# The MLP's down product as seven half-size block products

## The reference, cut to what matters

```python
h2 = rms_norm(x, norm_mlp[layer])
x = x + jnp.square(jax.nn.relu(h2 @ w_ff1[layer])) @ w_ff2[layer]
return rms_norm(x, norm_final)
```

## Time and profile before

| What | us |
|---|---|
| median of 3 runs | 1758.12 (1756.83 to 1758.76) |
| the profiled execution | 1756.69 |
| its span, first to last instruction | 1755.1 |
| TensorE matmul busy | 1740.4 (99%) |
| VectorE busy | 801.2 (46%) |
| ScalarE busy | 589.3 (34%) |
| GpSimd busy | 80.7 (5%) |

### The profile page before, as it was taken

One profiled execution on the slowest core, in us unless ns is written; L12 is line 12 of the kernel. 1 busy time (PEld: TensorE's weight loads), 2 busy tenths in 40 slices (PEclk: granted clock), 3 DMA queues, 4 the chain that ended last, 5 costly groups with the idle time before them and its releaser, 6 DMA issues.

```text
span 1755.1 us, 21871 instructions
## 1 busy us (share of the span) xinstructions
PE 1740.4 (99%) x8476; PEld 1275.0 (73%) x8476; DVE 801.2 (46%) x1160; ACT 589.3 (34%) x754; POOL 80.7 (5%) x148
## 2 busy tenths in 40 slices
PE   9999999999999999999999999999999999999998
PEld 7888888874444444444788877788888888888886
DVE  6323338453342424243672455566675544324423
ACT  5334433331212111122454534354532253113313
POOL 3000000000000000000020022200000000000000
PEclk9999999999999999999999999999999999999999
DMA  6222222858999999999314221222242222232232
GB/s 209 94 96 93 72 72 97 341 229 346 423 422 421 422 422 422 422 422 401 107 49 131 92 94 52 80 86 97 95 174 98 100 96 96 96 96 96 96 97 83
DMA packets 91169, 326.34 MB, mean 186 GB/s; under 512 B 8720, under 2 KB 9248, under 8 KB 66528
## 3 DMA queue, kind: packets, MB, share of 16 engines
q1 hardware_dynamic: 89328, 320.18, 48.1%
q0 software_dynamic: 1776, 5.26, 0.9%
HBM read 319.13 MB, written 6.29 MB: 185 GB/s over the span
## 4 chain that ended last, share of the span: by engine, by line
PE 97%; DVE 1%; ACT 1%; DMA 0%; issue 0%; SPq 0%; DVEq 0%; ACTq 0%
PE bank L2309 61%; PE bank L2640 13%; PE bank L2653 6%; PE bank L2548 3%; PE bank L2595 3%; PE bank L2334 3%; PE bank L2882 2%; PE bank L2820 1%; PE bank L2764 1%; PE bank L2841 1%; PE bank L2913 0%; PE bank L2511 0%; DMA w_stage<-in_w_in 0%; PE bank L2522 0%; PE bank L2919 0%
## 5 line engine op out<-in xcount | busy, mean ns | idle before, releaser
L2309 PE MATMUL bank<-act_hi,w_hi 128*128 128x512 f32 x992 | 389.7, 393 | 0.0
L2309 PE MATMUL bank<-act_hi,w_lo 128*128 128x512 f32 x992 | 386.3, 389 | 0.0
L2309 PE MATMUL bank<-act_lo,w_hi 128*128 128x512 f32 x992 | 386.2, 389 | 0.0
L1457 DVE TENSOR_TENSOR w_lo<-w_stage,w_hi 128x2048 fp32r<-128x2048 f32 x98 | 224.4, 2289 | 349.4 <-ACT w_hi L859 349.4
L859 ACT ACTIVATE w_hi<-w_stage 128x2048 fp32r<-128x2048 f32 x98 | 187.8, 1916 | 383.3 <-PE bank L2309 377.8
L2640 PE MATMUL bank<-ring,xgT 128*64 128x512 f32 x992 | 215.7, 592 | 0.2 <-ACT xgT L1078 0.2
L2309 PEld LDWEIGHTS bank<-act_hi,w_hi 128*128 128x128 f32 x992 | 186.3, 188 | 40.0 <-issue 2.5
L2309 PEld LDWEIGHTS bank<-act_hi,w_lo 128*128 128x128 f32 x992 | 186.2, 188 | 39.2
L2309 PEld LDWEIGHTS bank<-act_lo,w_hi 128*128 128x128 f32 x992 | 186.4, 188 | 37.6
L2640 PEld LDWEIGHTS bank<-ring,xgT 128*64 128x64 f32 x992 | 70.7, 137 | 141.5 <-issue 141.0
L2653 PE MATMUL bank<-ring,gatedT 128*64 128x512 f32 x512 | 113.4, 595 | 0.0
(11 more groups left out here) (430 smaller groups left out, 2035.7 us busy)
## 6 DMA issues: line engine op xcount, KB each, us to landing
ring<-in_w SPq DMA_DIRECT2D x188, 1024.0 KB, 12.0
w_stage<-in_w_in SPq DMA_DIRECT2D x45, 1024.0 KB, 5.0
w_stage<-in_w_ff SPq DMA_DIRECT2D x32, 1024.0 KB, 5.2
w_stage<-in_w_out SPq DMA_DIRECT2D x8, 1024.0 KB, 5.1
extra<-in_w SPq DMA_DIRECT2D x4, 1024.0 KB, 8.4
branch_gates<-gate_out POOLq DMA_DIRECT2D x16, 256.0 KB, 2.5
w_stage<-in_w_proj_gla SPq DMA_DIRECT2D x4, 1024.0 KB, 9.8
w_stage<-in_w_pg SPq DMA_DIRECT2D x3, 1024.0 KB, 5.1
```

The lines of the kernel that those rows point to most:

```text
L1457: dve.tensor_tensor(w_lo[s][:, 0:ktiles, :], w_stage[s][:, 0:ktiles, :], w_hi[s][:, 0:ktiles, :].bitcast(F32), ALU.subtract).then_inc(w_lo ...
L2309: ins = pe.matmul(gb[j][:, :], left, right, start=(kc == 0 and k == 0 and n_pass == 0), stop=(kc == g.chunks - 1 and k == g.ktiles - 1 and ...
```

## The change

The down product of each half is the product of A (512 tokens x 2048) and B (2048 x 1024). It's now cut in quarters: A into a11, a12 (tokens 0 to 255, hidden 0 to 1023 and 1024 to 2047) and a21, a22 (tokens 256 to 511), B likewise into b11, b12 (the first 1024 rows, columns 0 to 511 and 512 to 1023) and b21, b22. In place of eight products of quarters there are seven, in this order (PARTS = 7):

| part | left operand | right operand | bank pair, added into |
|---|---|---|---|
| 0 | a11 | b11 | gb[0:2], rows 0-255, first columns |
| 1 | a12 | b21 | mb[0:2], the same quarter |
| 2 | S2 = a21 + a22 - a11 | T2 = b22 - b12 + b11 | on top of part 0; rows 0-255, second columns |
| 3 | S1 = S2 + a11 | T1 = b12 - b11 | gb[2:4]; rows 256-511, second columns |
| 4 | S3 = a11 - a21 | T3 = b22 - b12 | on top of 2; rows 256-511, second columns |
| 5 | S4 = a12 - S2 | b22 | on top of 3; rows 0-255, second columns |
| 6 | a22 | T4 = b21 - T2 | on top of 4; rows 256-511, first columns |

Each part is two steps of one 1 MB weight block each (step v = 2 x part + kc, 14 steps a half), each step two tiles of 12 matmuls: 7 x 2 x 2 x 12 = 336 matmuls a half. After each part DVE adds its two banks into `x` (`add_part`), 14 additions a half.

- `hidden` now holds the squares in float32, written by DVE alone; ACT's squares are gone. Each part's left operand, 128 x 8 x 256, is split when it's needed (`part_split_hi` on ACT, `part_split_lo` on DVE) into a double buffer.
- The sums S1 to S4 are four DVE instructions of 128x2048 a half (`sum_three` in the up phase, the others in the down phase).
- The sums T1 to T4 are made of 1 MB blocks on GpSimd, ten instructions of 128x2048 a half (`summed_block`): sums 1 to 4 (for T2) in the up phase, 5 and 6 (T1), 7 and 8 (T3), 9 and 10 (T4) while the down product runs. The blocks that they need are loaded again, so a half loads 18 blocks for the down product where it loaded 8.
- Semaphores `lb_diff` and `gl_edge` are given up; their waits go by `const_dve` and `gl_dist`.
- At the end the halves of the final norm follow the order in which quarters are ready, and the last part holds only the first columns of row tiles 2 and 3.

```diff
+        part_bank = [(gb[0:2], mb[0:2], gb[0:2], gb[2:4], gb[0:2], gb[2:4], gb[0:2])[n] for n in range(PARTS)]
+        step_stage = (w_stage[0], w_stage[1], w_stage[0], b_one[1], b_sum[0], b_sum[1], w_stage[0], w_stage[1],
+                      b_one[1], b_one[0], b_one[1], b_one[0], b_sum[0], b_sum[1])
...
+                sp.wait_ge(w_lo_done, step(h, 1))
+                sp.dma_start(w_stage[1][:, :, :], weight_block(h, 1, 1, 1)).then_inc(w_loaded[1], 16)
+                sp.wait_ge(w_lo_done, step(h, 2))
+                sp.dma_start(w_stage[0][:, :, :], weight_block(h, 1, 1, 0)).then_inc(w_loaded[0], 16)
+                sp.wait_ge(w_lo_done, step(h, 3))
+                sp.dma_start(b_one[1][:, :, :], weight_block(h, 0, 0, 0)).then_inc(b_one_in[1], 16)
+                sp.wait_ge(part_low, PARTS * h + 3)
+                sp.wait_ge(hid_summed, 4 * h + S4)
+                sp.dma_start(b_one[0][:, :, :], weight_block(h, 0, 0, 1)).then_inc(b_one_in[0], 16)
...
+            def summed_block(out, left, right, op):
+
+                pool.tensor_tensor(out[:, :, :], left[:, :, :], right[:, :, :], op).then_inc(b_summed, 1)
...
+                for kc in (1, 0):
+                    pool.wait_ge(w_loaded[kc], stage0[kc] + (48, 32)[kc])
+                    summed_block(w_stage[kc], w_stage[kc], b_sum[kc], ALU.subtract)
+                for kc in range(2):
+                    pool.wait_ge(b_one_in[1 - kc], 16 * ((4, 5)[1 - kc] * h + (5, 4)[kc]))
+                    summed_block(b_one[1 - kc], b_sum[kc], b_one[1 - kc], ALU.subtract)
+                for kc in range(2):
+                    pool.wait_ge(w_loaded[kc], stage0[kc] + (64, 48)[kc])
+                    pool.wait_ge(w_lo_done, step(h, 4 + kc))
+                    summed_block(b_sum[kc], w_stage[kc], b_sum[kc], ALU.subtract)
...
+                act.wait_ge(pe_tiles, (down.chunk0 + v - 1) * 4)
+                act.activation(w_hi[v % 2][:, :, :], step_stage[v][:, :, :], ACT.Copy).then_inc(w_hi_done, 1)
...
+                step_split_lo(h, 1)
+                part_split_lo(h, 1)
+                step_split_lo(h, 2)
+                sum_two(h)
...
+                for n in range(PARTS - 2):
+                    step_split_lo(h, 2 * n + 3)
+                    part_split_lo(h, n + 2)
+                    add_part(h, n, 0)
+                    step_split_lo(h, 2 * n + 4)
+                    add_part(h, n, 1)
+                    if n == 0:
+                        sum_one(h)
+                    elif n == 1:
+                        sum_four(h)
...
+                for k in range(4):
+                    ka = 4 * kc + k
+                    for n_pass, (left, right) in enumerate(((a_hi, hi), (a_hi, lo), (a_lo, hi))):
+                        ins = pe.matmul(part_bank[n][j][:, :], left[:, ka, cols], right[:, k, :],
+                                        start=(part_first[n] and kc == 0 and k == 0 and n_pass == 0),
+                                        stop=(kc == 1 and k == 3 and n_pass == 2), skip_group_check=True)
+                ins.then_inc(pe_tiles, 2)
```

More of the change, by code:

```diff
@@ L35, with __init__ @@
 class Gemm:
-    def __init__(self, after, units, chunks, taker, ktiles=4):
+    def __init__(self, after, units, chunks, taker, ktiles=4, tiles=4):
         self.taker, self.after = taker, after
@@ L48, in __init__ @@
         self.chunk1 = self.chunk0 + units * chunks
-        self.tile1 = self.out[taker] = self.tile0 + 4 * units
+        self.tile1 = self.out[taker] = self.tile0 + tiles * units
 class Chain:
@@ L126, in two_blocks @@
         up = Gemm(last, FH // 512, 2, "act")
-        last = Gemm(up, 2, FH // 512, "dve")
+        last = Gemm(up, 2, PARTS, "dve", tiles=PARTS)
         g_ff.append((up, last))
@@ L689, in _ @@
             for t in range(NT):
-                for half, done, count in ((slice(512, D), n_xn, rows_count(6, t)), (slice(0, 512), last_left, NT + t + 1)):
+                for half, done, count in ((late(t), n_xn, rows_count(6, t)), (early(t), last_left, NT + t + 1)):
                     sp.wait_ge(done, count)
@@ L1387, in mlp_squares, with relu_unit @@
                                        accum_out=ssq[:, t:t + 1]))
-            def relu_unit(h, u, chunk):
+            def relu_unit(h, u):
+                up = g_ff[h][0]
                 for j in range(4):
[L1392 to L1402, removed]
+                    act.wait_ge(pe_tiles, (up.chunk0 + 2 * u + 1) * 4 + j + 1)
+                    if hid_count(h, u) + j >= 2:
+                        act.wait_ge(hid_sq, hid_count(h, u) + j - 1)
+                    act.activation(relu_t[j % 2][:, :], gb[j][:, :], ACT.Relu).then_inc(out_act, 1)
@@ L2233, in hidden_unit, with part_split_lo @@
                         .then_inc(hid_sq, 1)
[L2234 to L2239, removed]
+            def part_split_lo(h, n):
+                dve.wait_ge(part_high, PARTS * h + n + 1)
+                rest(part_lo[n % 2][:, :, :], part_operand[n], part_hi[n % 2][:, :, :]).then_inc(part_low, 1)
@@ L2241, in _, with sum_one, sum_four @@
+            def sum_one(h):
+                dve.wait_ge(hid_summed, 4 * h + S2)
+                dve.tensor_tensor(a11, s_two[:, :, :], a11, ALU.add).then_inc(hid_summed, 1)
+            def sum_four(h):
+                dve.wait_ge(part_low, PARTS * h + 2)
+                dve.tensor_tensor(a12, a12, s_two[:, :, :], ALU.subtract).then_inc(hid_summed, 1)
             for h, (up, down) in enumerate(g_ff):
                 split_lo(up.chunk0 + 1, 1)
[L2243 to L2246, removed]
@@ L2247, in _ @@
-                split_lo(down.chunk0, 0)
-                hidden_unit(h, up.units - 1)
-                split_lo(down.chunk0 + 1, 1)
+                for u in range(up.units):
+                    if u + 1 < up.units:
+                        split_lo(up.chunk0 + 2 * u + 2, 0)
+                    else:
+                        step_split_lo(h, 0)
+                    if u == 2:
+                        part_split_lo(h, 0)
+                        sum_three(h)
+                    hidden_unit(h, u)
+                    if u + 1 < up.units:
+                        split_lo(up.chunk0 + 2 * u + 3, 1)
@@ L2989, in _ @@
                 else:
-                    gemm(up, fm=True)
-                gemm(down, fm=False, ready=lambda kc, j, h=h, up=up: j == 0 and pe.wait_ge(
-                         hid_lo_done, h * 4 * up.units + 4 * (kc + 1)),
-                      a_hi=hid_hi, a_lo=hid_lo, base=tuple(range(0, FH // P, 4)))
+                    gemm(up, fm=True, ready=lambda kc, j, h=h: kc == 0 and pe.wait_ge(out_dve, added(h - 1, *last_add[j])))
+                for n in range(PARTS):
+                    pe.wait_ge(part_low, PARTS * h + n + 1)
+                    for kc in range(2):
+                        for j in range(2):
+                            part_passes(h, up, down, n, kc, j)
 _INS = ["x", "p", "g_mix", "w_in", "gm_ln_g", "gm_ln_b", "gm_w_sp", "gm_b_sp", "w_up_a", "hg_lb_param",
```

237 lines of the change are left out of this document (180 added, 57 removed).

## The result

The changed kernel takes 1781.6 us (median of 4 runs, 1779.06 to 1782.03) where the kernel before takes 1757.47 (4 runs, 1756.7 to 1758.76): a ratio of 1.0132, 95% interval 1.012 to 1.0144. It is 24.1 us slower; the forecast was 17.1 us slower.

The account below looks back on a forecast made before the run. TensorE, 97% of the chain, was taken as the bound. 1756.7 - 21.8 (matmuls) + 34.9 (collisions) + 4 (clock) = 1773.8 us, as a median 1775.2; range 1735.5 to 1794.

Parts of the forecast that it names:

- the likeliest case: GpSimd sums and two-input DVE instructions exclude each other, a sum taking 3.3 to 5.2 us: 1764 to 1794 us, chance 0.60.
- D: Time of one GpSimd block sum of 128x2048 in the down product: taken as 4.0 us, bounds 2.0 and 5.8.
- Matmuls removed: Down products of both halves: 96 matmuls fewer at 0.2267 us each, all on the path, 21.8 us saved.
- Work off the path: Operand splits, sums, additions and loads of the short down-product steps, and the tail: fits beside PE, 0 us.
- the tail: From the last matmul to the kernel's end: chain of 6.5 us kept, change 0, between -0.5 and +1 us.
- The collision: Down product: two-input DVE instructions and reading GpSimd sums wait for each other's end; 17.4 us stall a half, 34.9 in all.
- The formula, 6 D - 6.6 a half: Down product's stall in each half: 17.4 + 6 (D - 4.0) us; with the matmuls removed, 12 D - 35 us over both.
- The clock: PE's granted clock falls in long down-product stalls: 2 us for each of two, +4 us, between 0 and 11.
- (b): No exclusion for these sums, or DVE always first, so only the matmuls count: 1736.3 us, chance 0.15.
- (c): Exclusion, but a cheap sum (2.0 to 2.9 us) or a partial block: 1747 to 1758 us, chance 0.12.
- (d): A sum between, 2.9 to 3.3 us: 1758 to 1764 us, chance 0.06.
- (e): A sum dearer still, over 5.2 us, with long stalls at the lower clock: 1794 to 1805 us, chance 0.07.

Follow-up runs that it names:

- e1: Changed kernel with GpSimd's sums 5 to 10 of each half left out, only the semaphore raised: 1737.62 us, ratio 0.9886.
- e8: Changed kernel with the two small DVE instructions on 128x4 (row scale, reciprocal) moved before the up product's last unit of the first half: 1782.49 us, ratio 1.0137.
- e6: Changed kernel with filler matmuls put before the four waits of each half at which PE stood idle: 1775.94 us, ratio 1.0106.
- e3: Changed kernel with sums 5 to 10 made over the first half of each block only (128x1024): 1749.16 us, ratio 0.9952.
- e2: Changed kernel with each of sums 5 to 10 replaced by three GpSimd memsets of the same block, which read nothing: 1737.71 us, ratio 0.989.

## Why the prediction was right, and where its sizes were off

The direction and the mechanism were right. The stated range (1735.5 to 1794) holds faster as well as slower outcomes, so what decides is the likeliest case, exclusion with D between 3.3 and 5.2, and the experiments bear that one out. Its lower end was worked out a little too high: 12 x 3.3 - 35 = 4.6 gives 1763, not 1764.

**Matmuls removed, -21.8 us.** Right: with the late sums left out (e1) the two down phases run at 0.2267 us a matmul and the kernel gains 20.5 us, which is 21.8 less most of the longer tail.

**Work off the path, 0.** Right for the steps, splits, additions and loads: e1 has them all and no stall. Wrong in one term: the tail was put at 0, between -0.5 and +1, and measured +1.9 us. The step that failed is that two tiles would stand in line where four did. The last remainder, held behind ACT's four squares and the root's bias, is followed by four gain products (2.5 us) on DVE, and behind these still stand all four rows, one after the other, 2.85 us each for those with an addition; the last two rows are reached late.

**The collision.** Right in kind: exclusion for whole instructions, in turns, in both directions. Right in place for the second half: forecast 2.2, 7.1, 3.3, 0.8 and 3.9 us before steps 3, 4, 8, 9 and 10; measured idle 2.35, 5.83, 3.06, none and 3.31, together 14.6 for 17.3, and matmuls at the lower clock fill part of what is missing. In the first half the forecast had the order wrong at the start: it left out the small instruction behind sum_two, and the idle time of steps 3 and 4 stood as one stretch of 6.80 us before step 3. By e8 that order made no difference in time. That all the colliding rows of before were short on GpSimd's side was said to be the argument's weak point; the waits of 3.4 to 4.4 us beside each late sum closed it.

**The price of a sum, D.** Mis-sized: 4.0 us from two reading passes of the affine_select's slope, measured 4.59. By the forecast's own formula that is 0.59 x 12 = 7.1 us. The Trainium skill (GPSIMD Engine Reference, Performance versus the Vector engine) gives 4497 ns for a tensor_tensor add of this size; the trace has 4.59 us, 2% more.

**The formula, 6 D - 6.6 a half.** With the clock held up (e6) the phases lost 19.8 and 19.0 us, 19.4 in the mean, where the formula gives 20.9 at D = 4.59; with half sums (e3) they lost 5.9, where it gives 7.8. So the slope is borne out, (19.4 - 5.9) / (4.59 - 2.40) = 6.2 us for each us of a sum, and the constant is 1.5 to 2 us a half too high. Part of that is seen in the turns: one of a sum and one of a remainder took 4.4 + 2.15 us together, where the formula at D = 4.59 counts the lengths that each has alone, 4.59 + 2.29.

**The clock, +4 us, between 0 and 11.** Measured 3 to 6. The reason was right in part. Whether PE is late afterwards anyway decides what a slow stretch costs. And the length of the gap alone doesn't tell whether the clock falls: after about 3.3 us idle before step 10 it stayed at 1.00 in the second half of the changed kernel and in the first half of e8, and was at 0.50 in the second half of e8; after 2.35 us before step 3 it was at 0.50 (second half of the changed kernel, 1691.0 to 1694.0). What decides it wasn't tried.

In the spans of the profiled executions, the collisions net of the matmuls removed, forecast as 13.1 us, came out as 19.8 + 19.0 - 21.8 = 17.0; the clock, forecast as 4, as 2.6 (the 20.6 + 20.8 lost in the changed kernel's phases less e6's 19.8 + 19.0); the tail, forecast as 0, as 1.9; 0.9 is what the span's account left over. Together 22.4, and the medians are 24.1 apart, 1.7 more. That the error in D, 7.1 us, equals the whole miss of 7.0 is luck: the other errors (-3.2 for the formula, -1.4 for the clock, +1.9 for the tail, +0.9 and +1.7 for the rest) cancel.

**Rivals.** (b), no exclusion, fell by the turns in the trace and by e2; its number, 1736.3, is nearly that of e1, 1737.6, the kernel without the late sums. (c) and (d), a cheap sum, and (e), a dearer one, fell with 4.59 us. GpSimd's waiting never lasted over several DVE instructions.

## What to carry to other kernels

Work moved from a full engine to an idle one is only hidden if the two don't need the same port: here a sum of 4.59 us on GpSimd held VectorE up by 3.4 to 4.4 us, where the same sum costs 2.29 on VectorE itself, and a change that removed 22 us of matmuls came out 24 slower. Before such a move, look in the trace for places where the two engines already meet and read both lengths against the undisturbed ones. And when operands are cut smaller, count the cover of each step anew: a wait of 3.4 us cost nothing under chunks with 6.7 us to spare.

## What the runs showed of the hardware that was not expected

- A DVE tensor_scalar on 128x4 with a single SBUF input waited for a GpSimd sum to its end, 4.59 us for 0.16 (e8), while the bank additions (one input in PSUM, one in SBUF) beside sums kept their 0.74 us.
- The sum of a block with itself took 3.60 us on GpSimd, the sum of two different blocks 4.59, both 128x2048. Why wasn't tried.
- In the stretch shown, with instructions of both engines waiting, the port went to the other engine at each end (turns of 4.4 us for a sum, 2.15 for a remainder); where the small instruction had stood in DVE's turn, in the first half of the changed kernel, GpSimd got two sums in a row.
